# Forgetting attention: the scores of unit u+2 between the two heads' turns of unit u, the paged values' products in three parts, their probabilities copied first

## The reference

```
s = q . k / sqrt(d) + D_q - D_k          (D = cumsum of log f)
s = where(kpos <= qpos, s, NEG_INF)
p = softmax(s);  o = p @ v
```

## Time and profile before

| | us |
|---|---|
| median of three runs | 1810.51 (1808.78 to 1812.75) |
| the profiled execution | 1808.62 |
| its span, first to last instruction | 1806.8 |
| the attention stage, about | 186 (469 to 655) |

### The profile page before, as it was taken

The page is one execution under the profiler, slowest core; times in us unless marked ns, Lnnn a source line. Parts: engine busy times, 40 slices in busy tenths (PEclk is TensorE's granted clock), DMA queues, the critical chain, the costliest instruction groups (busy, mean ns, idle before and its releaser), DMA issues. The chain is left out here.

```text
span 1806.8 us, 27711 instructions
## 1 busy us (share of the span) xinstructions
PE 1588.7 (88%) x10583; PEld 1393.2 (77%) x10587; DVE 1038.2 (57%) x1730; ACT 625.1 (35%) x1112; POOL 745.0 (41%) x837
## 2 busy tenths in 40 slices
PE   4689988999688877899699569999999999699996
PEld 2568887899566655689577469999999999588874
DVE  1561008650355534455334496887777776669885
ACT  2432132231244433122223334443433343444352
POOL 0541013221000005686103378999999996000011
PEclk7899999999899888789799888999999999799998
DMA  8335531230311128442132201222222222795862
GB/s 320 127 125 184 175 99 62 77 104 18 122 62 38 39 81 230 118 119 69 67 137 94 82 33 60 82 87 72 78 79 72 73 80 85 238 292 177 282 237 96
DMA packets 136981, 210.98 MB, mean 117 GB/s; under 512 B 38756, under 2 KB 78484, under 8 KB 133522
## 3 DMA queue, kind: packets, MB, share of 16 engines
q1 hardware_dynamic: 134386, 200.31, 33.9%
q10 hardware_dynamic: 2464, 8.91, 1.3%
HBM read 166.14 MB, written 42.91 MB: 116 GB/s over the span
## 5 line engine op out<-in xcount | busy, mean ns | idle before, releaser
L2696 DVE SCALAR_TENSOR_TENSOR fu_tmp<-fu_zp,fu_cw,fu_tmp 128x1024 f32<-128x1024 f32 x88 | 150.6, 1712 | 76.0 <-ACT fu_tmp L2631 74.4
L2441 PE MATMUL fu_ps<-fu_thi,fu_wlo 128*128 128x272 f32 (+2 forms) x672 | 139.1, 288 | 0.0
L2441 PE MATMUL fu_ps<-fu_thi,fu_whi 128*128 128x272 f32 (+2 forms) x672 | 138.9, 288 | 0.0
L2441 PE MATMUL fu_ps<-fu_tlo,fu_whi 128*128 128x272 f32 (+2 forms) x672 | 138.9, 288 | 0.0
L3018 PE MATMUL fd_ps<-fd_bhi,fd_ahi 128*128 128x512 f32 x308 | 121.3, 394 | 19.2 <-DVE fd_blo L3129 19.2
L2473 POOL TENSOR_TENSOR fu_wlo<-fu_s,fu_whi 128x512 fp32r<-128x512 f32 x84 | 119.4, 1432 | 18.9 <-ACT fu_whi L2587 18.3
L2587 ACT ACTIVATE fu_whi<-fu_s 128x512 fp32r<-128x512 f32 x84 | 50.9, 629 | 215.7 <-PE fu_ps L2441 89.4
L3018 PE MATMUL fd_ps<-fd_bhi,fd_alo 128*128 128x512 f32 x308 | 121.2, 393 | 0.0
L3018 PE MATMUL fd_ps<-fd_blo,fd_ahi 128*128 128x512 f32 x308 | 121.1, 393 | 0.0
L2441 PE MATMUL fu_ps<-h_hi,fu_whi 128*128 128x272 f32 (+1 forms) x504 | 105.6, 291 | 15.4 <-POOL fu_wlo L2473 15.4
L2473 POOL TENSOR_TENSOR fu_wlo<-w_raw,fu_whi 128x512 fp32r<-128x512 f32 x67 | 109.8, 1641 | 9.7 <-ACT fu_whi L2587 9.7
(11 more groups left out here) (398 smaller groups left out, 4040.1 us busy)
## 6 DMA issues: line engine op xcount, KB each, us to landing
wa<-in_w_ada SPq DMA_DIRECT2D x24, 1024.0 KB, 5.6
w_raw<-in_w_up SPq DMA_DIRECT2D x88, 256.0 KB, 2.5
fd_b<-in_w_down SPq DMA_DIRECT2D x86, 256.0 KB, 3.7
fd_a<-scr_y SPq DMA_DIRECT2D x86, 256.0 KB, 3.5
scr_y<-fu_tmp SPq DMA_DIRECT2D x22, 544.0 KB, 4.4
fp_w<-in_w_fm SPq DMA_DIRECT2D x15, 512.0 KB, 3.6
scr_qkv<-fp_y SPq DMA_DIRECT2D x9, 512.0 KB, 2.9
dr_stg<-scr_qkv SPq DMA_DIRECT2D x8, 576.0 KB, 6.0
```

Of the source, the lines that this page charges most:

```text
L2441: last = pe.matmul(lane_of(q, o)[:, n, 0:size], w[:, o, kk], part(low, kk, slice(c, c + size)), start=(kk == 0 and m == 0), stop=(kk == HK ...
L2696: one = dve.scalar_tensor_tensor(yp, a, w, yp, ALU.mult, ALU.add)
```

## The change

`FIRST` becomes 1: the samples start one iteration earlier. `scores` runs two units ahead of `turn`, which now belongs to the same iteration and is called once for each head. `values_c` is called three times, once for each pair of heads. The new orders of iteration u:

- TensorE: `turn(u,0)`, `scores(u+2)`, `values_c` pair 0, `turn(u,1)`, `values_c` pair 1, on even u `values((u-2)/2)`, `scores_c` or `turn_c`, `values_c` pair 2.
- ScalarE: `spread_c`, copies of (u,0), `exp_c`, `exp(u+1,1)`, `exp(u+2,0)`, on odd u the outputs, copies of (u,1).
- VectorE: copies of (u,0), `scale(u+1,1)`, `maximum(u+2,0)`, `scale_c`, on odd u the outputs, copies of (u,1), `scale(u+2,0)`, `maximum(u+2,1)`, `maximum_c` or `decay_c`.

The buffers, the products, the number of instructions and the rule by which groups fall to ScalarE or VectorE stay as they are.

```diff
--- before.py
+++ after.py
@@ -1043,7 +1043,7 @@
             sem("ca_" + n) for n in "table_in clear q own_mm own_set dn s max p dg t pt v hi lo".split())
         page_in = [sem("ca_page_in0"), sem("ca_page_in1")]
         LOADS = 16 * (3 * NPAGE + 1)
-        FIRST = 2
+        FIRST = 1
         OUT = 512 - PAIRS * NSAMP
         rows_of = [slice(0, HD), slice(HD, P)]
         free = [(psO[1], rows_of[0]), (psO[0], rows_of[1])]
@@ -1091,9 +1091,14 @@
                 eng.wait_ge(o_act, 2 * q + hh + 1)
                 eng.tensor_tensor(K.h_lo[at], src, K.h_hi[at], ALU.subtract).then_inc(o_dve, 1)
 
-        def mine(u, dve):
-
-            return [n for n, g in enumerate(groups) if g[0] == u and on_dve[n] == dve]
+        def mine(u, hh, dve):
+
+            return [n for n, g in enumerate(groups) if g[0:2] == (u, hh) and on_dve[n] == dve]
+
+        def paged(u):
+
+            b, step = divmod(u - FIRST, 3)
+            return (b, step) if 0 <= b < NBATCH else (None, None)
 
         @block.sync
         def _(sp):
@@ -1150,17 +1155,16 @@
                 for hh in range(2):
                     pe.matmul(psS[hh][:, i * P:n], c16[:, 0:P], c16[:, P:2 * P], start=False, stop=True).then_inc(s_mm, 1)
 
-            def turn(u):
-                for hh in range(2):
-                    pe.wait_ge(dg_set, 2 * u + hh + 1)
-                    for b in range(0, u % NT + 1, 4):
-                        n = group_of[u, hh, b]
-                        if n >= 2:
-                            transposed(pe, n - 2)
-                        for x in range(groups[n][3]):
-                            last = pe.matmul(psT[n % 2][:, x, :], pb[:, u % 2, hh, (b + x) * P:(b + x + 1) * P], dg[:, u % 2, hh, :],
-                                             start=True, stop=True)
-                        last.then_inc(t_mm, 1)
+            def turn(u, hh):
+                pe.wait_ge(dg_set, 2 * u + hh + 1)
+                for b in range(0, u % NT + 1, 4):
+                    n = group_of[u, hh, b]
+                    if n >= 2:
+                        transposed(pe, n - 2)
+                    for x in range(groups[n][3]):
+                        last = pe.matmul(psT[n % 2][:, x, :], pb[:, u % 2, hh, (b + x) * P:(b + x + 1) * P], dg[:, u % 2, hh, :],
+                                         start=True, stop=True)
+                    last.then_inc(t_mm, 1)
 
             def values(q):
                 j, m = q // (NT // 2), q % (NT // 2)
@@ -1196,33 +1200,45 @@
                     pe.matmul(ps[rows, c // 2 * R:(c // 2 + 1) * R], pc[:, c * HD:(c + 1) * HD], dgc[:], start=True, stop=True)
                 pe.matmul(psO[1][0:SSEQ, NPAGE * R:(NPAGE + 1) * R], pc[:, PAST:KEYS], dgc[:], start=True, stop=True).then_inc(ca_t, 1)
 
-            def values_c(b):
+            def values_c(b, j):
                 pe.wait_ge(ca_pt, 3 * (b + 1))
-                for j in range(PAIRS):
-                    for c in range(NPAGE + 1):
-                        for e in range(2):
-                            h = 2 * j + e
-                            ps, rows = free[e]
-                            n = P if c < NPAGE else SSEQ
-                            v = (vp[:, b % 2, c] if c < NPAGE else vo[:, b % 2])[:, h * HD:(h + 1) * HD]
-                            o = OUT + j * NSAMP + b * SSEQ
-                            last = pe.matmul(ps[rows, o:o + SSEQ], v, ptc[0:n, c, h * SSEQ:(h + 1) * SSEQ],
-                                             start=(c == 0), stop=(c == NPAGE))
-                last.then_inc(ca_v, 1)
+                for c in range(NPAGE + 1):
+                    for e in range(2):
+                        h = 2 * j + e
+                        ps, rows = free[e]
+                        n = P if c < NPAGE else SSEQ
+                        v = (vp[:, b % 2, c] if c < NPAGE else vo[:, b % 2])[:, h * HD:(h + 1) * HD]
+                        o = OUT + j * NSAMP + b * SSEQ
+                        last = pe.matmul(ps[rows, o:o + SSEQ], v, ptc[0:n, c, h * SSEQ:(h + 1) * SSEQ],
+                                         start=(c == 0), stop=(c == NPAGE))
+                if j == PAIRS - 1:
+                    last.then_inc(ca_v, 1)
 
             pe.wait_ge(c16_set, 1)
             pe.matmul(psO[1][0:R, 0:NSAMP], K.cst[64:64 + H_C, C_ROW48:C_ROW48 + R], K.rows[64:64 + H_C, SEQ:TOK], start=True, stop=True)\
                 .then_inc(own_mm, 1)
-            for u in range(UNITS + 2):
+            scores(0)
+            scores(1)
+            for u in range(UNITS + 1):
+                b, step = paged(u)
                 if u < UNITS:
-                    scores(u)
-                if 1 <= u <= UNITS:
-                    turn(u - 1)
-                if u >= 3 and u % 2 == 1:
-                    values((u - 3) // 2)
-                b, step = divmod(u - FIRST, 3)
-                if 0 <= b < NBATCH:
-                    (scores_c, turn_c, values_c)[step](b)
+                    turn(u, 0)
+                if u + 2 < UNITS:
+                    scores(u + 2)
+                if step == 2:
+                    values_c(b, 0)
+                if u < UNITS:
+                    turn(u, 1)
+                if step == 2:
+                    values_c(b, 1)
+                if u >= 2 and u % 2 == 0:
+                    values((u - 2) // 2)
+                if step == 0:
+                    scores_c(b)
+                if step == 1:
+                    turn_c(b)
+                if step == 2:
+                    values_c(b, 2)
 
         @block.scalar
         def _(act):
@@ -1244,22 +1260,26 @@
                         .then_inc(ca_pt, 1)
                 act.activation(ptc[0:SSEQ, NPAGE], psO[1][0:SSEQ, NPAGE * R:(NPAGE + 1) * R], ACT.Copy).then_inc(ca_pt, 1)
 
+            exp(0, 0)
+            exp(0, 1)
+            exp(1, 0)
             for u in range(UNITS + 2):
-                before = mine(u - 1, False) if 0 < u <= UNITS else []
-                half = len(before) // 2
-                for hh in range(2):
-                    if u < UNITS:
-                        exp(u, hh)
-                    for n in (before[:half], before[half:])[hh]:
-                        spread(act, n)
-                if (u - FIRST) % 3 == 2 and 0 <= (u - FIRST) // 3 < NBATCH:
-                    spread_c((u - FIRST) // 3)
+                b, step = paged(u)
+                if step == 2:
+                    spread_c(b)
+                for n in mine(u, 0, False):
+                    spread(act, n)
+                if step == 1:
+                    exp_c(b)
+                if u + 1 < UNITS:
+                    exp(u + 1, 1)
+                if u + 2 < UNITS:
+                    exp(u + 2, 0)
                 if u >= 3 and u % 2 == 1:
                     output(act, (u - 3) // 2, 0)
                     output(act, (u - 3) // 2, 1)
-                b, step = divmod(u - FIRST, 3)
-                if step == 0 and 0 <= b < NBATCH:
-                    exp_c(b)
+                for n in mine(u, 1, False):
+                    spread(act, n)
             act.wait_ge(ca_v, NBATCH)
             for ps, rows in free:
                 act.activation(K.h_hi[rows, 5:8, SEQ:TOK], ps[rows, OUT:512].rearrange("p (j t) -> p j t", j=PAIRS), ACT.Copy)\
@@ -1312,27 +1332,36 @@
             chain.link(dve.tensor_tensor(own48[:], psO[1][0:R, 0:NSAMP].rearrange("p (b s) -> p b s", s=SSEQ), caus, ALU.add))
             dve.sem_inc(own_set, 1)
             one = K.cst[0:R, C_TRI + P - 1:C_TRI + P].broadcast_to([R, PAST])
+            maximum(0, 0)
+            maximum(0, 1)
+            scale(0, 0)
+            scale(0, 1)
+            maximum(1, 0)
+            scale(1, 0)
+            maximum(1, 1)
             for u in range(UNITS + 2):
-                b, step = divmod(u - FIRST, 3)
-                if u < UNITS:
-                    maximum(u, 0)
-                    maximum(u, 1)
-                if step == 1 and 0 <= b < NBATCH:
+                b, step = paged(u)
+                for n in mine(u, 0, True):
+                    spread(dve, n)
+                if u + 1 < UNITS:
+                    scale(u + 1, 1)
+                if u + 2 < UNITS:
+                    maximum(u + 2, 0)
+                if step == 1:
                     scale_c(b)
-                if 1 <= u <= UNITS:
-                    for n in mine(u - 1, True):
-                        spread(dve, n)
-                if u < UNITS:
-                    scale(u, 0)
-                    scale(u, 1)
                 if u >= 3 and u % 2 == 1:
                     output(dve, (u - 3) // 2, 0)
                     output(dve, (u - 3) // 2, 1)
-                if step == 0 and 0 <= b < NBATCH:
+                for n in mine(u, 1, True):
+                    spread(dve, n)
+                if u + 2 < UNITS:
+                    scale(u + 2, 0)
+                    maximum(u + 2, 1)
+                if step == 0:
                     if b == 0:
                         decay_c(0)
```

(2 more changed lines are left out.)

## The result

The changed kernel is slower: median 1817.92 us of six runs (1814.76 to 1822.68) against 1808.20 for the kernel before, timed beside it, ratio 1.0067 (95% interval 1.0050 to 1.0084). In the experiments it was timed again, again beside the kernel before: 1819.14 against 1806.01, 1.0081 (1.0066 to 1.0096). The forecast was no change, 1810.5.

The account below looks back on a forecast made before the run. The prediction took TensorE to bound the attention stage, with 23.3 us of removable idle and 12.5 us of clock loss. It summed +3.6 idle and -3.6 clock to no change, 1810.5 us, range 1800 to 1820.

Parts of the forecast that it names:

- (a): Paged products: with the probabilities' copy first on ScalarE, TensorE's 7.4 us of waits go, except 0.9 us at the end.
- (b): Scores two units ahead: transposes' 13.8 us of waits go, VectorE's chain brings waits to 26.9; scores' waits under 15 refute it.
- (c): Stage's start: scores(2) waits for max(1,1), 1.2 us later than before; the longer half clock costs +0.6 us.
- (d): TensorE's clock after the start: four falls of 4.5 us, 18 us low, costing 8.3 us.
- The sum: Attention stage: +3.6 us of idle and -3.6 us from the clock give 0, no change; chance 0.43.
- R2: Slower: the chain holds scores(u+3) back, and seven waits above 1.8 us each drop the clock; +9.1, 1819.6 us, chance 0.23.
- R1: TensorE's waits move but its clock stays full after the start; -8.3, 1802.2 us, chance 0.28.
- R3: Exps and scales are covered and TensorE waits only at the ends; -32, 1778 us, chance 0.06.

Follow-up runs that it names:

- e11: Kernel before, with only the copy of the paged probabilities (`spread_c`) moved first in ScalarE's iteration: 1789.14 us, ratio 0.9909 to the kernel before.
- e2: Changed kernel with max(u+2,1) on VectorE taken ahead of both scale(u+2,0) and the outputs: 1793.81 us, ratio 0.9934 to the kernel before.
- e7: Changed kernel with max(u+2,1) ahead of scale(u+2,0) on VectorE, outputs left where they were: ratio 1.0017 to the kernel before.
- e8: Changed kernel with only VectorE's outputs moved behind max(u+2,1): ratio 0.9941 to the kernel before.
- e1: Changed kernel without further edits, timed and profiled a second time beside the kernel before: 1819.14 us, ratio 1.0081.
- e10: Changed kernel with VectorE's maxima ahead of scales and outputs, 40 filler products at the start, ScalarE's and VectorE's queues reordered by need: 1778.66 us, ratio 0.9845.
- e12: Kernel before with only the change's paged half (early copy, products in three parts), plus 40 filler products at the start: ratio 0.9896 to the kernel before.

## Why the prediction was wrong, point by point

- **(a)** Right: 0.8 us of the copy's waits is left, and 0.9 was forecast. What it is worth was asked in the old order alone: there, by e11, it is the best line of the change.
- **(b)** Right in mechanism, a little high in size: 26.9 us of waits forecast beside the start's, 22.6 and 22.5 measured. For u=11 4.0 was forecast and 3.3 measured, for u=17 4.2 and 3.4. The place was half wrong: only 11.6 us stand at the scores, below the 15 that I had set as the mark against (b); the rest stands at the paged diagonal and at the transposes, ahead of the scores in TensorE's queue, where the same late exps and copies are awaited. e2, e7 and e8 show that VectorE's order is the cause all the same.
- **(c)** The step that failed by size: the start at the low clock was put at "+0.6 us". It lasted 17.6 and 13.8 us in place of 10.2, which at 0.46 is 3.4 and 1.7 us: 2.8 and 1.1 more than forecast.
- **(d)** The step that failed and decided: "I take four falls", "4.5 us each", 18 us. Measured behind the start were five falls in each profile, 27.3 and 40.9 us, which is 12.6 and 18.8 us of loss, not 8.3. With (c), the forecast had a gain of 3.6 us from the clock; in the two profiles there was a loss of 3.4 and 7.9. I had priced each wait alone against the 1.8 us that were harmless before. In the changed kernel the clock also fell behind shorter ones, and once it was low, stretches of 13.7 us came, for which the trace before had no example.
- **What (d) read off the trace before.** It was too clean. Of the five falls there, those at 588.9 and 633.3 begin in the scores, 0.2 and 1.1 us behind the paged products, not in them. And before 633.3 stood two waits near each other, one of them a transposes' wait of 1.8 us, so it can't be said that none of the ten took part in a fall:

```profile
628.10 1.58 PE L1161 MATMUL fa_psT<-fa_dg,fa_p 128*128 128x128 f32 x12 [1.81 <-ACT fa_pt L1080]
630.54 0.41 PE L1209 MATMUL fa_psO<-ca_pt,w_raw 128*64 128x8 f32 x8 [0.86 <-ACT ca_pt L1245]
```

- **What brings a fall** stays open. Waits near each other stand before falls (1.44 and 1.98, 1.25 and 0.92), but a second one isn't needed: in e8 the clock fell at 596.1 behind 1.44 us alone, with the paged scores and paged transposes around it. Nor are a long wait and small products near each other enough: in e11 a wait of 1.67 us, 1.5 us ahead of the 72 products, left the clock full.
- **The sum** with measured terms: idle -0.7 and -0.8, clock +3.4 and +7.9: +2.7 and +7.1 us, where the stage grew by 4.9 and 7.9. Of the first, 2.2 us stay unexplained by the factor of 0.46; they are in TensorE's busy time, which grew by 6.3.
- **The rivals.** R2 came true in kind: the chain holds the scores back, and the clock makes it slower. Its price, +9.1 us, is near the +9.7 and +13.1 between the medians, but in part by luck: it was made of 3.6 us more idle and seven falls of 5.4 us, and measured were 0.7 and 0.8 us less idle, five falls that were longer in e1, and the longer start. It had 0.23; the forecast of no change, 0.43, was too sure of (d). Both times lie inside the stated 1800 to 1820, at its upper end. The page that spoke for R2 (the Trainium skill, TensorE: Matmul & The Clock Gate, "A second HAM failure mode: psum-queue depth-cycling") was set aside for one row of before, where the waits stood alone. The runs agree with the page in part: the changed kernel's two traces have five stretches each, with waits of 0.8 to 2.0 us beside them; but in e11 ten waits for the two transposes' tiles, up to 1.8 us, left the clock full.
- R1 and R3 fell for this kernel. What R1 described, a full clock after the start, was had by e10, e11 and e12. R3's time of 1778 was reached by e10 (1778.66), with other queue orders and a filler.

## What to carry to other kernels

Where a single buffer passes between two engines, the reader that frees it goes ahead of everything in its queue that waits for a third engine: here a maximum behind an output cost 1.3 to 1.4% of the kernel. When a reordering moves idle without removing it, the clock can still take its price: look at what stands around each new wait, not at its length alone, and take an interval for it that holds the difference between two executions of one kernel. And try each half of a two-part change alone, since one half here gained 0.5%, a single call of it in the old order 0.9%, and the other half lost 1.0%.

## What the runs showed of the hardware that was not expected

Ninety small bf16 products put where TensorE waited anyway made the kernel 0.8 to 0.9% faster: low clock after the start 10.2 us in place of 27.3 and 40.9. With the same waits to 0.2 us, two executions of the changed kernel differed by 13.6 us in that low clock. Ten waits of the transposes, up to 1.8 us, left the clock full (e11), while in the kernel before the clock fell 1.9 us behind a wait of 0.42 us, with the 8-column products between the earlier trace rows; without that wait, the same products in e11 brought no fall.
